# The prompt's row softmax between the pieces of panels 14 to 17, and half of the selected-value pages on GpSimd's queue

## What is computed

```python
z = x @ w_in                       # prompt 512 rows + 8 sample rows, 18 panels of 128 columns
u_conv, q_nsa, kv_nsa, g_nsa, qkv_moba, u_pool = split(z)
# B: o_nsa  = g0 * o_cmp + g1 * o_sel + g2 * o_win      (4 heads, one K/V head for each branch)
#    o_cmp: softmax over compressed blocks; o_sel: top-16 blocks of 64 rows; o_win: window of 512
# C: o_moba: own block of 256 keys and the top 3 others  (4 heads)
# prompt: keys are the prompt's own rows; sample: keys and values are in paged caches,
#    16 pages of 128 rows for each of the 8 samples
mix = concat([y_conv, o_nsa, o_moba, y_pool]) @ w_out
x = layer_norm(ALPHA * x + mix);  x = layer_norm(ALPHA * x + square(relu(x @ w_up)) @ w_down)
```

## Time and profile before

| | |
|---|---|
| median of 3 runs | 884.84 us (884.17 to 888.94) |
| the profiled execution | 885.0 us, span 883.2 us |
| busy: PE, DVE, ACT, POOL | 795.7, 457.6, 289.4, 146.9 us |
| mean granted clock of PE | 0.956 |
| panels 14 to 17, from 159.8 to 232.6 us | 72.8 us, PE busy 63.8, clock 1.00 |
| to the first column step, 267.7 us | 35.1 us, PE busy 19.4, clock 0.68 |
| units mixed with columns, to 396.6 us | 128.9 us, PE busy 115.0, clock 0.90 |
| tail to the output projection, 426.8 us | 30.2 us, PE busy 23.0, clock 0.89 |
| output projection and feed-forward, to 883.2 us | 456.4 us, PE busy 431.5, clock 0.98 |

### The profile page before, as it was taken

The page is one execution under the profiler, slowest core; times in us unless marked ns, Lnnn a source line. Parts: engine busy times, 40 slices in busy tenths (PEclk is TensorE's granted clock), DMA queues, the critical chain, the costliest instruction groups (busy, mean ns, idle before and its releaser), DMA issues.

```text
span 883.2 us, 17247 instructions
## 1 busy us (share of the span) xinstructions
PE 795.7 (90%) x6793; PEld 684.7 (78%) x6793; DVE 457.6 (52%) x832; ACT 289.4 (33%) x569; POOL 146.9 (17%) x148
## 2 busy tenths in 40 slices
PE   6999989978767798896989899999999999999983
PEld 6988877755323355552889899999999999999982
DVE  4289955465635443343476855553355335533445
ACT  4322244444454112123243445431243113411123
POOL 0003570000000000000045575100011001100073
PEclk9999999999878699998999999999999999999997
DMA  8546653536725687640123332333223332233202
GB/s 322 158 133 156 182 167 119 193 129 206 241 67 177 195 261 217 186 162 25 48 72 121 118 91 78 96 97 96 78 91 106 89 93 80 89 113 83 91 4 96
DMA packets 73291, 113.20 MB, mean 128 GB/s; under 512 B 25177, under 2 KB 42202, under 8 KB 72538
## 3 DMA queue, kind: packets, MB, share of 16 engines
q1 hardware_dynamic: 63994, 109.99, 40.2%
q10 hardware_dynamic: 9216, 2.10, 1.1%
HBM read 107.63 MB, written 6.52 MB: 129 GB/s over the span
## 4 chain that ended last, share of the span: by engine, by line
PE 70%; DVE 15%; issue 7%; ACT 4%; ACTq 2%; DMA 1%; POOL 1%; SPq 0%; DVEq 0%; POOLq 0%
PE psum L653 50%; DVE yc L1459 4%; PE psum L731 2%; PE psum L967 2%; PE psum L763 2%; PE psum L662 2%; PE psum L706 2%; PE psum L913 2%; PE psum L902 1%; PE psum L734 1%; DVE nmR L1484 1%; DVE wL L1397 1%; ACTq L1127 1%; ACT psum L1137 1%; PE psum L950 1%
## 5 line engine op out<-in xcount | busy, mean ns | idle before, releaser
L1397 DVE TENSOR_TENSOR wL<-raw,wH 128x1024 fp32r<-128x1024 f32 x90 | 118.3, 1314 | 112.7 <-ACT wH L1057 112.7
L1057 ACT ACTIVATE wH<-raw 128x1024 fp32r<-128x1024 f32 x90 | 93.7, 1042 | 128.5 <-PE psum L653 124.8
L653 PE MATMUL psum<-oxH,wH 128*128 128x260 f32 (+1 forms) x512 | 105.6, 288 | 3.8 <-DVE wL L1397 3.7
L653 PE MATMUL psum<-opH,wH 128*128 128x260 f32 (+1 forms) x416 | 89.1, 296 | 21.1 <-DVE opL L1393 8.1
L653 PE MATMUL psum<-hidH,wH 128*128 128x260 f32 x512 | 103.9, 284 | 2.6 <-issue 2.6
L653 PE MATMUL psum<-oxH,wL 128*128 128x260 f32 (+1 forms) x512 | 104.4, 285 | 0.0
L653 PE MATMUL psum<-oxL,wH 128*128 128x260 f32 (+1 forms) x512 | 104.0, 284 | 0.0
L653 PE MATMUL psum<-hidL,wH 128*128 128x260 f32 x512 | 103.7, 284 | 0.0
L653 PE MATMUL psum<-hidH,wL 128*128 128x260 f32 x512 | 103.7, 284 | 0.0
L653 PEld LDWEIGHTS psum<-opH,wH 128*128 128x128 f32 (+1 forms) x416 | 65.4, 192 | 29.6 <-issue 12.4
L653 PE MATMUL psum<-opH,wL 128*128 128x260 f32 (+1 forms) x416 | 85.5, 288 | 0.0
(11 more groups left out here) (343 smaller groups left out, 1136.7 us busy)
## 6 DMA issues: line engine op xcount, KB each, us to landing
raw<-in_panels SPq DMA_DIRECT2D x89, 512.0 KB, 3.6
moba_lo<-in_moba_pages SPq DMA_DIRECT2D x64, 256.0 KB, 3.5
moba_hi<-in_moba_pages SPq DMA_DIRECT2D x64, 256.0 KB, 3.6
nsa_ring<-in_nsa_pages SPq DMA_DIRECT2D x128, 96.0 KB, 2.2
xres<-in_xT SPq DMA_DIRECT2D x8, 260.0 KB, 6.3
xres<-in_xT SPq DMA_DIRECT2D x1, 2080.0 KB, 8.8
out_y<-xres SPq DMA_DIRECT2D x8, 260.0 KB, 2.1
selV<-in_selv_pages SPq DMA_DIRECT2D x64, 32.0 KB, 2.7
```

The source lines that it names most:

```text
L653: last = mm(out[0:M, hf, 0:cols], w, x[:, k, hf * HALF:hf * HALF + cols], start=(t == 0 and j == 0), stop=(t == KT - 1 and j == 2))
L1057: fn(wH[:, n % NW].rearrange("p a b -> p (a b)")[:, 0:m], raw[:, n % NRAW, 0:m], ACT.Copy).then_inc(h_done, 1)
L1397: tt(wL[:, n % NW].rearrange("p a b -> p (a b)")[:, 0:m], raw[:, n % NRAW, 0:m], wH[:, n % NW].rearrange("p a b -> p (a b)")[:, 0:m].bitca ...
```

## The change

`ATT_PANEL` goes from 15 to 14, and 28 row steps lie between panels 14 and 17 where 20 lay between 15 and 17. Panel 14 is cut in four with the last compression (`kv` 8) and `csc` in its middle; rows 0 to 3 stand behind its evacuation without pieces between. In panels 15 to 17 each k-tile is a piece, one row behind each, and the evacuation stands ahead of the last row. 12 decode units lie there instead of 10. Both `lse` follow each other and so do both `lset`; DVE's preparation is a step of its own (`prep`). In the merged part `comba`'s second half, `own`, `fina` and the second half of `combm` move back against their neighbours, and ACT takes its exponentials of the combine steps in the second halves. The split of the second output panel comes ahead of the last column instead of behind it. The selected-value pages of samples 1, 3, 5 and 7 are issued by POOL, each group after a given value step, those of the even samples by SP; ACT issues none.

```diff
-ATT_PANEL = 15
-ROW_PIECES = (7, 7, 6)
-MU1, UNIT = 10, 4.4
+ATT_PANEL = 14
+ROW_PIECES = (4, 8, 8, 8)
+MU1, UNIT = 12, 4.4
...
-        if i + 1 < N_PANELS and i + 1 != OUT0:
+        if i + 1 < N_PANELS and i + 1 not in (OUT0, OUT0 + 1):
...
-        out += spread([s for q in range(n) for s in (("mm", i, q, n), ("row", first + q))], extras)
-        return out + [("evac", i)]
+        atoms = [s for q in range(n) for s in (("mm", i, q, n), ("row", first + q))]
+        if i == ATT_PANEL:
+            rows_ = [s for s in atoms if s[0] == "row"]
+            mms = [s for s in atoms if s[0] == "mm"]
+            return out + mms[:2] + [("kv", B), ("csc", 0)] + mms[2:] + [("zcols", 0), ("evac", i)] + spread(rows_, extras)
+        return out + spread(atoms[:-1] + [("evac", i), atoms[-1]], extras)
...
-    extras = {15: [("ctr", 0), ("zrow", 0), ("win", 0), ("cimp", 0), ("mu", 0)] + M(1, 2),
-              16: M(2, 4) + [("zrow", 1)] + M(4, 6),
-              17: M(6, MU1)}
+    extras = {14: [("ctr", 0), ("zrow", 0), ("win", 0)],
+              15: [("cimp", 0), ("mu", 0)] + M(1, 4),
+              16: M(4, 6) + [("zrow", 1)] + M(6, 8),
+              17: M(8, MU1)}
...
-    rows = [(0.5 + 0.8 * n, ("row", NR0 + n)) for n in range(NR - NR0)]
-    rows += [(0.3, ("lse", 0)), (5.5, ("lset", 0)), (7, ("lse", 1)), (13, ("lset", 1))]
+    rows = []
+    head = [(0, ("out_z", 0)), (0, ("prep", 0)), (0.3, ("zrow", 2)), (0.4, ("lse", 0)), (0.4, ("lse", 1)), (0.5, ("vrow", 0)), (0.6, ("vrow", 1)),
+            (2.5, ("lset", 0)), (2.6, ("lset", 1)), (2.7, ("own", 0)), (4, ("msplit", 0)), (4, ("msplit", 1))]
...
-    join = [(9 + 2 * k, ("stat", k)) for k in range(5)] + [(18.5, ("comba", 0)), (20, ("comba", 1)), (29, ("backa", 0))]
+    join = [(8 + 2 * k, ("stat", k)) for k in range(5)] + [(17.2, ("comba", 0)), (21.2, ("comba", 1)), (26, ("backa", 0))]
...
-    last = [(end, ("statm", 0)), (end + 0.1, ("combm", 0)), (end + 0.2, ("combm", 1)), (end + 12, ("backm", 0)), (end + 15.5, ("mpv", 0)), (end + 19, ("finm", 0)),
+    last = [(end, ("statm", 0)), (end + 0.1, ("combm", 0)), (end + 7, ("combm", 1)), (end + 12, ("backm", 0)), (end + 15.5, ("mpv", 0)), (end + 19, ("finm", 0)),
...
@@ SP
-                elif kind == "selv" and n % 2 == 0:
+                elif kind == "selv" and n // 4 % 2 == 0:
@@ ACT
-                elif kind == "selv" and n % 2 == 1:
-                    for p in range(n * 4, n * 4 + 4):
-                        v = act.value_load(page_ids[0:1, p:p + 1])
-                        act.dma_start(selV[p // PAGES][:, p % PAGES, :],
...
-                elif kind == "comba" and n == 0:
+                elif kind == "comba" and n == 1:
...
-                elif kind == "combm" and n == 0:
+                elif kind == "combm" and n == 1:
@@ POOL
+                if kind == "selv" and n // 4 % 2 == 1:
+                    if n == 4:
+                        pool.wait_ge(ids_in, 16)
+                        pool.wait_ge(mm_done, N_IN_PANELS)
+                    pool.wait_ge(mp_mm, MU1 + n // 2 - 2)
+                    for p in range(n * 4, n * 4 + 4):
+                        v = pool.value_load(page_ids[0:1, p:p + 1])
+                        pool.dma_start(selV[p // PAGES][:, p % PAGES, :],
+                                       a["selv_pages"][bass.ds(v, 1)].rearrange("a p n -> (a p) n")).then_inc(selv_in[p // PAGES], 16)
@@ DVE
-                    ts(gT[:, :, :], gT[:, :, :], 0.5, 0.5, ALU.mult, ALU.add).then_inc(gate_done, 1)
+                    chain(ts(gT[:, :, :], gT[:, :, :], 0.5, 0.5, ALU.mult, ALU.add))
+                    chain(ts(gT[:, :, :], gT[:, :, :], 1e-30, None, ALU.max))
+                    nc.vector.reciprocal(gT[:, :, :], gT[:, :, :]).then_inc(gate_done, 1)
```

More of the change, by code:

```diff
@@ L175, in timeline @@
             tl += [("cpw", 0), ("pool", 1), ("load_lo", 0)]
-        if i == 14:
-            tl += [("csc", 0), ("zcols", 0)]
-    head = [(0, ("out_z", 0)), (0.1, ("zrow", 2)), (0.2, ("own", 0)), (1.5, ("vrow", 0)), (2.5, ("vrow", 1)), (3, ("msplit", 0)), (3, ("msplit", 1))]
-    rows = [(0.5 + 0.8 * n, ("row", NR0 + n)) for n in range(NR - NR0)]
-    rows += [(0.3, ("lse", 0)), (5.5, ("lset", 0)), (7, ("lse", 1)), (13, ("lset", 1))]
+    rows = []
+    head = [(0, ("out_z", 0)), (0, ("prep", 0)), (0.3, ("zrow", 2)), (0.4, ("lse", 0)), (0.4, ("lse", 1)), (0.5, ("vrow", 0)), (0.6, ("vrow", 1)),
+            (2.5, ("lset", 0)), (2.6, ("lset", 1)), (2.7, ("own", 0)), (4, ("msplit", 0)), (4, ("msplit", 1))]
     units = []
@@ L183, in timeline @@
         at_ = 1 + UNIT * (u - MU1)
-        units += [(at_, ("mu", u)), (at_ + UNIT / 2, ("mp", u - 1))]
+        units += [(at_, ("mu", u)), (at_ + 0.5 * UNIT, ("mp", u - 1))]
         units += [(at_, ("selv", k)) for k in (2 * (u - MU1), 2 * (u - MU1) + 1) if k < 4 * B]
     end = 1 + UNIT * (MU + 1 - MU1)
-    join = [(9 + 2 * k, ("stat", k)) for k in range(5)] + [(18.5, ("comba", 0)), (20, ("comba", 1)), (29, ("backa", 0))]
+    join = [(8 + 2 * k, ("stat", k)) for k in range(5)] + [(17.2, ("comba", 0)), (21.2, ("comba", 1)), (26, ("backa", 0))]
     for b in range(B):
-        at_ = 33 + (end - 40) / B * b
+        at_ = 29 + (end - 38) / B * b
         join += [(at_ - 3, ("psc", b))] + [(at_ + 1.7 * c, ("st", b, c)) for c in range(3)] + [(at_ + 6, ("spv", b))]
@@ L192, in timeline @@
             join.append((at_ + 6, ("load_panel", OUT0 + b)))
-    join += [(end, ("msplit", 2)), (end, ("msplit", 3)), (end + 1, ("load_x", 1)), (end + 1, ("split", OUT0)), (end + 2, ("fina", 0)),
-             (end + 6, ("msplit", 4)), (end + 6, ("msplit", 5))]
+    join += [(end, ("msplit", 2)), (end, ("msplit", 3)), (end + 1, ("load_x", 1)), (end + 1, ("split", OUT0)), (end + 20, ("split", OUT0 + 1)), (end + 9, ("fina", 0)),
+             (end + 13, ("msplit", 4)), (end + 13, ("msplit", 5))]
     cols = []
     for n in range(NC + 1):
-        at_ = 8 + (end - 10) / NCN * n if n < NCN else end + 1 + 2.5 * (n - NCN)
+        at_ = 5 + (end - 8) / NCN * n if n < NCN else end + 1 + 2.5 * (n - NCN)
         if n < NC:
@@ L1326, in _ @@
                     tt(pb[:, :], pb[:, :], x, ALU.subtract).then_inc(pool_d, 1)
-                if kind == "xsum":
+                if kind == "selv" and n // 4 % 2 == 1:
[7 more added lines that the diff above has]
+                                       a["selv_pages"][bass.ds(v, 1)].rearrange("a p n -> (a p) n")).then_inc(selv_in[p // PAGES], 16)
+                elif kind == "xsum":
                     if n == 1:
@@ L1484, in _ @@
                         red(nmR[:, i, c:c + 2], psum[:, b:b + 2, 0:P * (i + 1)], AX.X, ALU.max, negate=True).then_inc(max_done, 1)
+                elif kind == "prep":
+                    dve.wait_ge(mm_done, N_IN_PANELS)
+                    nc.vector.tensor_copy(pick[:, :], cst[:, C_PICK:C_PICK + 16])
+                    ts(shift[:, :, :].rearrange("p a b -> p (a b)"), spread(cst[:, C_PICK], 2 * T), 0.0, None, ALU.mult).then_inc(pick_done, 1)
                 elif kind == "lse":
@@ L1487, in _ @@
                     L = lR[:, :, lo:hi]
-                    if n == 0:
-                        dve.wait_ge(mm_done, N_IN_PANELS)
-                        nc.vector.tensor_copy(pick[:, :], cst[:, C_PICK:C_PICK + 16])
-                        ts(shift[:, :, :].rearrange("p a b -> p (a b)"), spread(cst[:, C_PICK], 2 * T), 0.0, None, ALU.mult).then_inc(pick_done, 1)
-                        chain(ts(gT[:, :, :], gT[:, :, :], 1e-30, None, ALU.max))
-                        chain(nc.vector.reciprocal(gT[:, :, :], gT[:, :, :]))
                     dve.wait_ge(exp_done, (NR0, NR)[n])
                     if n == 0:
+                        dve.wait_ge(gate_done, 1)
                         chain(ts(L, L, 1e-30, None, ALU.max))
```

4 lines of the change are left out of this document (removed).

## The result

The changed kernel takes **850.8 us** (median of 4 runs, 850.5 to 856.6) against 884.8 us before: ratio 0.962, 95% interval 0.957 to 0.967. The forecast was 856 us, its own sum before a lump was given back 850.9.

What follows compares the result with a forecast made beforehand. PE, partly idle or slow between 159.8 and 426.8 us, was taken as the bound. 254.5 + 115.0 + 23.2 + 456.4, plus 1.8 outside the span, gave 850.9; 4.8 given back made 856 us, range 847 to 873 (8 in 10).

Steps and rivals of the forecast that it cites:

- a lump: Half of 9.6 us of middle-stage wait gains, 4.8 us, added back because what is late next could not be read.
- pages: Stage 3: taking selected-value page issues off ACT removes 3.9 us of waits, 3.0 of low clock and 2.5 around own products.
- tail: Before the output projection: 6.67 us sampled-output wait and 2.2 of low clock go, 1.9 of new waits come; 23.2 us.
- evacuations: Waits for panel evacuations go: 4.0 us for panels 16 and 17, 2.81 us behind panel 17.
- Row 27: Last row step, end of stage 1: ends on PE at 232.6 + 10.7 - 4.0 + 4.6 = 243.9 us.
- To the first column step: From row 27 to the first column step: 10.6 us, both logarithms behind one table load, reaching 254.5 us against 267.7.
- Stage 3: Decode units mixed with column steps: 128.9 us falls to 115.0 by one unit less, fewer waits and less low clock.
- case D: Whole kernel: all gains go through, nothing given back, with a shorter tail: 846 to 850 us; chance 0.13.
- Rival A: Row pipeline becomes the bound: DVE's order loses 0.3 us on 24 rows and the clock falls: 868 us; chance 0.2.
- Rival C: Stage 2's waits reappear at the first column and the combine chain bounds the tail: 880 us; with mixtures, chance 0.08.
- Rival B: POOL's pages come late, eating the 29 us gain from 2.1 us a page; 914 us at 2.57; chance 0.09.
- 64p + 3 - 109: How many us late POOL's last selected-value page is when each page costs p us.

Runs made afterwards that it cites:

- before_pool_tail: The kernel before with GpSimd issuing the pages and the new tail order, without the row steps' new place: 867.5 us, ratio 0.978.
- try_order: The changed kernel with steps moved in stage 1 and stage 3, by order alone, nothing added: 845.3 us, ratio 0.956.
- after_old_tail: The changed kernel with the old order at its tail (sampled output, combine's second half and its exponent): 857.8 us, ratio 0.967.

## Why the prediction was right

**The stages and their causes were right.** The earlier trace rows held: long single waits with nothing to hide behind are the ones that a new order can remove. The four gains were undone one at a time, and each came back: pages 10 to 12 us (9.4 forecast), tail 7.8 (7.0), row steps 12 to 15 (14.5 forecast, 13.2 and 1.3), and, as a part of the last, evacuations 12 (6.8).

**Row 27 at 242.5 for 243.9 is right by parts that miss, and that is luck.** Stage 1 has to be counted from panel 14's start: 84.4 us (158.10 to 242.54) for a forecast of 84.1 (243.9 - 159.8), so the 1.4 us by which the mark is early come from the 1.7 us ahead of panel 14 and not from stage 1. I took 10.7 us more work, 4.0 off, 4.6 of new waits. Idle time of PE fell from 9.0 to 5.2 us, 3.8 less where I had 0.6 more. Busy time grew by 15.4 us (63.84 to 79.25), of which 0.08 x 79.3 = 6.3 us is the low clock that I had not priced: two stretches, among the sparse rows 0 to 3 and behind the importance chain. They stand in every profile of this order. The work alone grew by 9.1. So the work was mis-sized by 1.6 us, the waits by 4.4 and the clock by 6.3, and the sum by 0.3.

**The one new wait that I followed by rows came at its place and at half its size**: panel 16's split ahead of the importance chain and unit 0. I forecast 1.7 us more; the wait is 1.7 us in all, and 0.8 of it stood there before. What stands behind it, 5 us at a clock of 0.54, I missed.

**To the first column step**: 10.1 us for 10.6, with one table load of 1.28 us in front of both logarithms. The Trainium skill (ScalarE: Activation LUTs, What ACT_TABLE_LOAD costs) adds its figure of about 2.7 us up from 1283 ns for the load and 1380 ns of draining. The trace agrees with the first part (1.28 us) and shows nothing of the second: the load starts at 245.84, 0.02 us after the end of the copy ahead of it, and the logarithm at 247.13, 0.01 us after the load.

**Stage 3** came to 116.7 for 115.0. Against before, the low clock costs 6 us less, as forecast (6.2), and one unit less is in it, but PE is idle for 9.7 us instead of 13.9, 4.2 less where I had 6.4. The experiments show besides that its terms were in part at another place. Of the page issues' price 7.1 us lie here and 3.2 ahead of the first column, where the copy of `shift` stands behind them. The step that failed is the list of what stands behind an issue on ACT: I had read it from the waits of before alone, and not from ACT's order in the new kernel, where these steps are packed closer. The combine's wait stayed, as said, with 3.9 us for 3.3, and a wait of 2.2 us for unit 13 came that I did not have; it is the 2.2 us that are missing in the idle time.

**What was given back, 4.8 us, was the wrong step.** I had no mechanism for it, only that what is late next could not be read. What did come late was 2.2 us at unit 13; each forecast stage lies within 2 us. It moved the forecast from 850.9 to 856; the true time lay at the edge between the forecast's own band and case D (0.13), which was undervalued.

**Rival A** (the row pipeline is the bound) did not come about: from 190 us on stage 1 has full clock, and the rows' longest wait is 0.4 us. **Rival C** falls with the runs that undo each half.

**Rival B** (pages late) had the right arithmetic and a price that does not apply. The page costs 0.90 us; I had taken 1.1, between 0.72 and 2.57. With dearer pages the kernel follows 64p + 3 - 109 within 4 us, and by the line through the two runs it loses the whole gain from 2.1 us a page, as forecast. But the sentence ahead of it, that up to 1.9 us a page would be free by the lead of the last group, was wrong: a queue that falls behind in its first group carries that into the last, and by the same line the free price ends at 1.6. The sentence on SP was too sure as well: its eight pages in a row are covered in the changed kernel, but in four variants a unit waited 0.4 to 2.6 us for its pages. Against the rule of the Trainium skill (SBUF — State Buffer, SBUF: two separate sides), by which VectorE's use of the shared port starves the descriptors of GpSimd's DMAs, the issues keep their 0.53 us and land in 3.0 us, while DVE is at work for half of the time. Even its two scalings with both operands in SBUF, 1.16 and 0.68 us from 284.23 to 285.99, leave the issues at 284.57, 285.48 and 286.39 at their distance of 0.90 to 0.91 us. The case that the section describes, a copy from SBUF to SBUF in a mode that takes both ports, hardly occurs here, so the rule is not refuted.

## What to carry to other kernels

Price a wait together with the clock behind it: removing 7.8 us of evacuation waits was worth 12 us, and the low stretch of 5 us behind a 1.7 us wait cost 2.3 us, more than the wait. One profile does not show that price, since the same wait was followed by the low clock in one execution and not in another: look at several, and put it in the range.

Before two profiles are compared from a mark on, see that the mark is the same row in both. Here 1.7 us of the first stretch's gain lay ahead of it.

When an issuing step leaves an engine, list from the new order everything that stood behind it, since a part of the price was on a chain (`shift`) that the old profile showed as something else's wait. For a queue of transfers compare its whole work with the whole time until the last read; the lead of a single group says too much.

Where every term of a sum has its mechanism, do not take off a lump without one; put that doubt in the range.

## What the hardware showed that was not expected

- GpSimd issues a page transfer of 32 KB every 0.90 us (0.53 busy), against 0.72 on ACT's queue, and six more readings of the page number do not change it.
- A small operation of GpSimd costs its neighbours more than its own time: 0.71 us for 128 x 190 numbers made the page 1.39 us dearer, since the issue behind it starts 0.96 us after its end.
- The same wait in the same order of steps leaves the clock at its full level in one execution and is followed by the lower one in another: 2.24 us for an evacuation (clock 1.00 in 212 to 220 us of before, 0.66 in 215 to 225 of `before_pool_tail`), and 1.90 us at 145.8 us (1.00 in the changed kernel, 0.72 before).
- Two kernels that are the same up to there differ by up to 4.6 us at a row near 70 us (66.51 in `try_order`, 71.11 in `after_old_tail`), so that only intervals between rows tell a few us apart in single profiles.
